# A two-block network on one core: products in passes, a new entrance, and reordered closing norms

## The reference, cut to what matters

```python
# first block
hn = rmsnorm(concat(meta, x), norm1_g)
u, q, k, v, g_ssm, g_att = split(hn @ w_in)            # 1024 -> 512 + 3*512 + 2*1024
y_ssm = s5_mixer(u, ...)                               # 32 groups, 64 complex states each
q, k = rmsnorm(q), rmsnorm(k)
y_att = rmsnorm(diff_attention(q, k, v, lam, slopes))
h = h + (sigmoid(g_ssm) * (y_ssm @ w_ssm_out) + sigmoid(g_att) * (y_att @ w_att_out)) @ w_o
up = rmsnorm(h, norm2_g) @ w_up                        # 1024 -> 2 * 2816
h = h + (gelu(causal_conv3(up_a)) * up_b) @ w_down
# second block, on the 256 tokens of x
z = rms_norm(h, norm_mix) @ w_in_2                     # nine parts
ya, yb, yc = rglru(...), hgrn2(...), moba(...)
y = concat(rms_norm(ya), yb, rms_norm(yc))
x = x + y @ w_out_2
x = x + relu(rms_norm(x, norm_mlp) @ w_ff1) ** 2 @ w_ff2
return rms_norm(x, norm_final)
```

## Time and profile before

| | |
|---|---|
| median of 3 runs | 732.13 us (732.03, 732.13, 1547.2) |
| profiled execution | 735.88 us, of which the span of the core 734.1 us |
| TensorE busy | 706.6 us (96%), 6152 products and as many weight loads |
| VectorE busy | 537.2 us (73%) |
| ScalarE busy | 386.8 us (53%) |
| weights and inputs read | 113.69 MB, 16 DMA engines 48% busy with SP's queue |

### The profile page before, as it was taken

How to read it: one execution, slowest core, us unless ns; L and a number is a source line. 1 busy time by engine, 2 the same in 40 slices (tenths; PEclk the granted TensorE clock), 3 DMA queues, 4 the chain that set the end, 5 groups by cost and what they waited for, 6 DMA issues and landing times.

```text
span 734.1 us, 14582 instructions
## 1 busy us (share of the span) xinstructions
PE 706.6 (96%) x6152; PEld 663.5 (90%) x6152; DVE 537.2 (73%) x954; ACT 386.8 (53%) x587; POOL 24.3 (3%) x50
## 2 busy tenths in 40 slices
PE   6999999999999999999999999999889999999996
PEld 4988998888999999999999889888779998998995
DVE  5899798556978877776777889965767665666653
ACT  6487368366365454444446664587654434434431
POOL 3010000000000000000000320000000000000000
PEclk9999999999999999999999999999999999999999
DMA  8751153133555555555655553333346565565541
GB/s 241 207 171 59 59 172 117 60 112 119 172 173 173 185 200 190 173 177 196 199 175 173 179 172 116 116 115 116 115 125 194 190 210 172 184 215 175 179 165 57
DMA packets 94700, 115.66 MB, mean 158 GB/s; under 512 B 7971, under 2 KB 83932, under 8 KB 94636
## 3 DMA queue, kind: packets, MB, share of 16 engines
q1 hardware_dynamic: 94244, 114.51, 48.2%
q0 software_dynamic: 128, 0.13, 0.1%
q10 hardware_dynamic: 264, 0.10, 0.1%
HBM read 113.69 MB, written 1.05 MB: 156 GB/s over the span
## 4 chain that ended last, share of the span: by engine, by line
PE 78%; DVE 10%; ACT 7%; issue 3%; DMA 1%; SPq 0%; DVEq 0%; ACTq 0%
PE psum L1805 17%; PE psum L1806 16%; PE psum L1807 16%; PE psum L2344 4%; PE psum L2342 4%; PE psum L2343 4%; DVE w_lo L1081 4%; ACT w_hi L500 3%; PE psum L2111 2%; PE psum L2113 2%; PE psum L2109 2%; PE psum L1917 1%; PE psum L1952 1%; DMA xtok<-in_x_dram 1%; PE psum L2167 1%
## 5 line engine op out<-in xcount | busy, mean ns | idle before, releaser
L1081 DVE TENSOR_TENSOR w_lo<-w_raw,w_hi 128x2048 fp32r<-128x2048 f32 x105 | 239.4, 2288 | 72.0 <-ACT w_hi L500 71.8
L500 ACT ACTIVATE w_hi<-w_raw 128x2048 fp32r<-128x2048 f32 x105 | 199.0, 1906 | 54.4 <-PE psum L2344 36.6
L1805 PE MATMUL psum<-x2n_hi,w_hi 128*128 128x256 f32 x400 | 114.5, 286 | 2.6 <-DVE x2n_lo L1532 1.3
L1806 PE MATMUL psum<-x2n_lo,w_hi 128*128 128x256 f32 x400 | 112.0, 280 | 0.0
L1807 PE MATMUL psum<-x2n_hi,w_lo 128*128 128x256 f32 x400 | 111.9, 280 | 0.0
L1805 PE MATMUL psum<-hs_hi,w_hi 128*128 128x256 f32 (+1 forms) x352 | 99.5, 283 | 0.0
L1806 PE MATMUL psum<-hs_lo,w_hi 128*128 128x256 f32 (+1 forms) x352 | 99.1, 281 | 0.0
L1807 PE MATMUL psum<-hs_hi,w_lo 128*128 128x256 f32 (+1 forms) x352 | 98.9, 281 | 0.0
L1805 PEld LDWEIGHTS psum<-x2n_hi,w_hi 128*128 128x128 f32 x400 | 75.3, 188 | 5.9 <-DVE x2n_lo L1532 2.3
L1807 PEld LDWEIGHTS psum<-x2n_hi,w_lo 128*128 128x128 f32 x400 | 76.1, 190 | 0.0
L1806 PEld LDWEIGHTS psum<-x2n_lo,w_hi 128*128 128x128 f32 x400 | 75.2, 188 | 0.6
(11 more groups left out here) (439 smaller groups left out, 1520.8 us busy)
## 6 DMA issues: line engine op xcount, KB each, us to landing
w_raw<-in_w_ff_dram SPq DMA_DIRECT2D x32, 1024.0 KB, 5.3
w_raw<-in_w_in_dram SPq DMA_DIRECT2D x27, 1024.0 KB, 5.3
w_raw<-in_w_up_dram SPq DMA_DIRECT2D x22, 1024.0 KB, 5.1
w_raw<-in_w_down_dram SPq DMA_DIRECT2D x11, 1024.0 KB, 4.9
w_raw<-in_w_o_dram SPq DMA_DIRECT2D x4, 1024.0 KB, 5.4
w_raw<-in_w_out_dram SPq DMA_DIRECT2D x4, 1024.0 KB, 5.2
w_raw<-in_w_ssm_out_dram SPq DMA_DIRECT2D x2, 1024.0 KB, 5.1
w_raw<-in_w_att_out_dram SPq DMA_DIRECT2D x2, 1024.0 KB, 5.0
```

What stands on the lines that cost most here:

```text
L500: A.activation(w_hi[:, u % NW, :], raw[:, u % NRAW, :], ACT.Copy).then_inc(sem("hi_ready"), 1)
L1081: V.tensor_tensor(w_lo[:, u % NRAW, :], raw[:, u % NRAW, :], w_hi[:, u % NW, :].bitcast(F32), ALU.subtract).then_inc(sem("lo_ready"), 1)
L1805: T.matmul(out_, lh, rh, start=start, stop=False)
L1806: T.matmul(out_, lh, rl, start=False, stop=False)
```

## The change

1. **Passes.** `unit()`, `down()` and `ff2()` run through all slices with high x high, then all with high weight x low activation, then all with low weight x high activation. The wait for `lo_ready` moves from the start of the unit to the third pass of its first group; at the start stands `hi_ready`. Where an activation is awaited, the first pass waits for its high half slice by slice, the second for its low half. `out_first` keeps the old order.
2. **Entrance.** SP loads both halves of x before those of unit 0. ScalarE makes the squares of the 256 tokens (`x_square`), VectorE the copies out of PSUM (`x_meta`, `x_pair`). Unit 0 is done in two halves of its contraction, each over both groups. TensorE gets products of the identity with itself that nobody reads, three before the meta tokens and eight before the first unit (`keep_warm`). The table of Sqrt is loaded first, the exponentials of `log_dt` follow the norm, and `s5_angles` follows the scaling of `u`.
3. **Closing norms.** VectorE scales the four `mo` slices first, starts the reciprocal of `rst2` behind two of the `ycat_lo` slices, and makes the `xc` slices of `ycat_lo` before it scales `hgo`; ScalarE takes the second Silu behind the `xc` slices; TensorE runs `ya_stat` ahead of `hg_bc`.

```diff
@@ sync
             for h in range(2):
                 c = slice(512 * h, 512 * h + 512)
                 for t in range(2):
                     sp.dma_start(xtok[:, 1 + t, c], x[0, P * t:P * t + P, c]).then_inc(sem(f"x_in{h}"), 16)
+            for h in range(2):
                 sp.dma_start(raw[:, 0, 1024 * h:1024 * h + 1024].rearrange("p (k n) -> p k n", k=4),
...
@@ scalar, entrance
-            x_pair(0)
+            act.wait_ge(sem("constants"), CONSTANTS["small"])
+            A.activation(small[:, 1, 8:9], eps_col, ACT.Sqrt)
+            x_square(1, 0)
+            x_square(2, 0)
...
+            for kt in range(4):
+                x_high(kt)
             first_half(0)
+            for kt in range(4, KD):
+                x_high(kt)
+            first_half(1)
+            done[0] = 1
+            x_square(1, 1)
+            x_square(2, 1)
+            split_to(2)
+            act.wait_ge(sem("x_sum"), 1)
+            A.activation(small[:, 1, 0:3], small[:, 0, 8:11], ACT.Sqrt, bias=eps_col,
...
@@ vector, entrance
+            x_meta()
+            for i in range(4):
+                x_pair(i)
+            for kt in range(4):
+                xn_low(kt)
             first_half(0)
...
+            split_to(2)
+            dve.wait_ge(sem("x_rms"), 6)
+            scaled("u", 0, uT, 0)
+            s5_angles()
             s5_denominator()
-            dve.wait_ge(sem("x_rms"), 2)
-            scaled("u", 0, uT, 0)
             s5_lambda()
...
@@ tensor, unit
-                if un:
-                    pe.wait_ge(sem("lo_ready"), un + 1)
-                else:
-                    pe.wait_ge(sem("first_lo"), 1)
+                pe.wait_ge(sem("hi_ready" if un else "first_hi"), un + 1)
...
+                    for kt in range(kk):
+                        if ready and fresh:
+                            pe.wait_ge(sem(ready + "_hi"), kt + 1)
...
+                        product(wh, ah, kt, first=kt == 0)
+                    for kt in range(kk):
+                        if ready and fresh:
+                            pe.wait_ge(sem(ready + "_lo"), kt + 1)
+                        product(wh, al, kt)
+                    if fresh:
+                        pe.wait_ge(sem("lo_ready" if un else "first_lo"), un + 1)
+                    for kt in range(kk):
...
+                        last = product(wl, ah, kt, final=kt == kk - 1)
                     last.then_inc(sem("group_done"), 1)
...
+            def keep_warm(n):
...
+                for _ in range(n):
+                    T.matmul(banks[0][:, 0:P], ident[:], ident[:], start=True, stop=True)
...
+            keep_warm(8)
+            first_unit()
...
@@ vector, closing norms
             for p_ in range(4):
                 STT(out=mo[:, p_, :], in0=mo[:, p_, :], scalar=col("att_norm", p_), in1=rst3[:, :],
                     op0=ALU.mult, op1=ALU.mult).then_inc(sem("yc"), 1)
-                if p_:
-                    y_low(p_ - 1, 3 + p_, mo[:, p_ - 1, :])
-            y_low(3, 7, mo[:, 3, :])
+            for p_ in range(2):
+                y_low(p_, 4 + p_, mo[:, p_, :])
             dve.wait_ge(sem("ya_rms"), 1)
-            seq(V.reciprocal(rst2[:, :], rst2[:, :]))
+            mark(V.reciprocal(rst2[:, :], rst2[:, :]))
+            for p_ in range(2, 4):
+                y_low(p_, 4 + p_, mo[:, p_, :])
...
```

More of the change, by code:

```diff
@@ L1741, in _ @@
             for m in range(2):
+                y_low(4 + m, m, xc[:, m, :])
+            for m in range(2):
                 dve.wait_ge(sem("hg_bc"), m + 1)
@@ L1866, in _ @@
                     pe.wait_ge(sem(f"x_in{kt // 4}"), 32)
-                need(pe, "hT_copy", kt // 2 - 1)
-                to_features(kt).then_inc(sem("xT"), 1)
+                for t in range(2):
+                    c = 256 * (kt % 2) + P * t
+                    last = T.transpose(banks[4 + kt // 2][:, c:c + P], xtok[:, 1 + t, P * kt:P * kt + P], ident[:])
+                if kt % 2:
+                    last.then_inc(sem("xT"), 1)
             param_cols(1, "ssm_in", 4)
@@ L1878, in token_rows, with first_unit @@
                 return last
[L1880 removed]
+            def first_unit():
+                wh, wl = (w[:, 0, :].rearrange("p (k n) -> p k n", k=KD) for w in (w_hi, w_lo))
+                for h in range(2):
+                    for m in range(2):
+                        for n_, (w, x) in enumerate(((wh, xn_hi), (wh, xn_lo), (wl, xn_hi))):
+                            if m == 0 and n_ != 1:
+                                pe.wait_ge(sem((("first_hi", "hi_ready")[h], "", ("first_lo", "lo_ready")[h])[n_]), 1)
+                            for kt in range(4 * h, 4 * h + 4):
+                                if m == 0 and n_ < 2:
+                                    pe.wait_ge(sem(("xn_hi", "xn_lo")[n_]), kt + 1)
+                                last = T.matmul(banks[m][:, 0:TOK], w[:, kt, P * m:P * m + P], x[:, kt, :],
+                                                start=(kt == 0 and n_ == 0), stop=(kt == KD - 1 and n_ == 2))
+                        if h == 1:
+                            last.then_inc(sem("group_done"), 1)
+            keep_warm(8)
+            first_unit()
             pe.wait_ge(sem("C_ready"), 2)
@@ L2088, in _ @@
             for i in range(2):
-                unit("att_out", i, (yatt_hi, yatt_lo, 0, NQ), 4, ready=None if i else "yatt_lo")
+                unit("att_out", i, (yatt_hi, yatt_lo, 0, NQ), 4, ready=None if i else "yatt")
             for i in range(4):
-                unit("w_o", i, (mix_hi, mix_lo, 0, NQ), 8, ready=None if i else "mix_lo")
+                unit("w_o", i, (mix_hi, mix_lo, 0, NQ), 8, ready=None if i else "mix")
             def h1_stat():
@@ L2252, in yc_stat @@
                              stop=(p_ == 3)).then_inc(sem("yc_stat"), 1)
-            unit("hg_f", 0, x2n, 8, ready="x2n_lo")
+            unit("hg_f", 0, x2n, 8, ready="x2n")
             x2_stat()
@@ L2348, in ff2, with product @@
-                if not final:
-                    last.then_inc(sem("acc_unit_done"), 1)
+                def product(u_, w, kt, t, h, z=False):
+                    return T.matmul(banks[4 + 2 * t + h][:, :], u_[:, i % 2, kt, P * t:P * t + P],
+                                    w[:, kt, 512 * h:512 * h + 512], start=False, stop=z, skip_group_check=True)
+                pe.wait_ge(sem("hi_ready"), un + 1)
+                pe.wait_ge(sem("u_hi"), 2 * i + 2)
+                if final:
+                    pe.wait_ge(sem("u_lo"), 2 * i + 2)
+                    pe.wait_ge(sem("lo_ready"), un + 1)
+                    for t in range(2):
+                        for n_, (u_, w) in enumerate(((u_hi, wh), (u_lo, wh), (u_hi, wl))):
+                            for kt in range(2):
+                                for h in range(2):
+                                    last = product(u_, w, kt, t, h, n_ == 2 and kt == 1)
+                        last.then_inc(sem("ff2_done"), 1)
+                    return
@@ new lines, in ff2 @@
+                for n_, (u_, w) in enumerate(((u_hi, wh), (u_lo, wh), (u_hi, wl))):
+                    if n_ == 1:
+                        pe.wait_ge(sem("u_lo"), 2 * i + 2)
+                    if n_ == 2:
+                        pe.wait_ge(sem("lo_ready"), un + 1)
+                    for kt in range(2):
+                        for t in range(2):
+                            for h in range(2):
+                                last = product(u_, w, kt, t, h)
+                last.then_inc(sem("acc_unit_done"), 1)
```

163 lines of the change are left out of this document (63 added, 100 removed).

## The result

The changed kernel takes 738.22 us (median of 7 runs, 737.28 to 740.39) against 735.36 us for the kernel before. The ratio is **1.0059, 95% interval 1.0033 to 1.0085**: slower by 0.6%, far inside the 2%. Two of the six runs of the kernel before in this ratio are the quick ones of the prediction's base (732.03 and 732.13); the other four have a mean of 735.5, and against these the changed kernel's mean of 738.68 is 0.44% slower. Its profiled execution takes 739.99 us with a span of 738.2, against 735.88 and 734.1 before: +4.1 us.

What follows compares the result with a forecast made beforehand. TensorE, busy for 96% of the span, was taken as the bound; entrance +2.7, handovers +2.1 and closing norms -1.45 gave +3.4 us, from a run median of 732.13 to 735.5 us, range 727.5 to 739.5.

Steps and rivals of the forecast that it cites:

- the base: Starting time of the forecast: the runs' median, 732.13 us, taken as 3.75 us below the profiled execution's 735.88.
- rival A: Pace of 256-column products: passes lead them into the faster spacing, up to -10 us, giving 725.5 to 730; chance 0.16.
- Pace and count: TensorE's products throughout: passes keep the number of products and weight loads, and the spacing stays; 0 us.
- Order behind the norm: Entrance: VectorE's list 2.8 us later from unit 2's low half, so TensorE reaches unit `q` 1 later by 2.7 us.
- rival B: Hidden entrance: unseen slack or an early clock rise makes the entrance cost 0 to 1 us, sum 732 to 733.5; chance 0.22.
- Identity products: Ahead of meta tokens and unit 0: unit 0 starts later but ends at 22.0, against 22.1 before; 0 us.
- Handovers: Between stages: 17 products left behind the last high half; `mix` +0.8, `x3` +0.9, `x2n` +0.3, others +0.1; sum +2.1 us.
- Closing norms: Output projection: the last `ycat_hi` and the chain behind it, to TensorE's restart, come earlier; -1.45 us, bounds -0.5 and -2.5.
- Rival C: Transposes between units `q` 0 and `q` 1: clock falls to 1.2 GHz, +1.8 us and slower transposes, 737.5 to 740; chance 0.13.
- signs of being wrong: Unit `q` 1 before 53 us, one spacing only of 256-column products, or groups behind `mix` and `x3` ending no later.

Runs made afterwards that it cites:

- combo: Changed kernel with the old product order in the first group of six slice-by-slice units, and angles before scaling `u`, `rbc` copy behind the sines; ratio 0.9939.
- passes: Kernel before with only the products in passes (`unit`, `down`, `ff2`), old entrance and old closing norms; ratio 1.0058.
- slices: Changed kernel with the first group of the six units whose activation comes slice by slice in the old order, three products per slice; ratio 0.9966.
- angles: Changed kernel with VectorE's angles ahead of the scaling of `u` and ScalarE's copy of `rbc` behind the two sines; ratio 1.0024.
- norms: Kernel before with only the reordered closing norms (`y_low`, `hg_g`, `ya_stat`); ratio 0.9976.
- after: The changed kernel itself, with all three parts of the change, against the kernel before; 738.22 us, ratio 1.0059.
- entr: Kernel before with only the new entrance, everything ahead of unit `u` 1; ratio 1.0005.
- warm: Changed kernel with two unread products ahead of each wait for a high half, from the third on, in the first group of `hg_f`; ratio 1.0033.
- fill3: Changed kernel with unread products ahead of waits in three sparse groups, in `hg_f`, `ff1` and `w_o` (30 products); ratio 1.0023.
- pair: Changed kernel with first and second product of a slice together in the six slice-by-slice first groups, third pass behind all slices; ratio 1.0009.
- both: The kernel `combo` with six products per slice, including the unit's second group, in the first unit of `hg_f` and `ff1`; ratio 0.9934 to the kernel before.

## Why the prediction came out as it did

**The direction and the size of the change were about right, the number was not.** I had +3.4 us on the profiled execution: 739.3. It took 739.99. In the ratio, +0.46% lies inside the interval of the measured +0.59%. But I put the forecast at 735.5 us, and that is 2.7 us under the median of 738.22.

**The step that failed is the base**: "The runs' median lies 3.75 us lower (732.13)". It came from three runs of which two happened to be among the quickest of this kernel. Of 85 later runs of the kernel before, 11 lie under 733.3 us, and the medians are 735.3 to 735.8, 0.1 to 0.6 us under the profiled execution and not 3.75. With the base at these medians the same +3.4 us gives about 739. As I wrote it, the forecast is the time that the kernel before really has (735.36), so it says "no change" where the runs show +0.6%. What makes a quick run is probably the pace of rival A, in another way than I had it. Low-half pass of a `down` unit in the changed kernel and in `combo` (TensorE):
```profile
356.37 2.05 PE L2148 MATMUL psum<-ff_lo,w_hi 128*128 128x256 f32 x16
358.25 0.99 PE L2148 MATMUL psum<-ff_hi,w_lo 128*128 128x256 f32 x7
```
```profile
366.45 1.98 PE L2161 MATMUL psum<-ff_lo,w_hi 128*128 128x256 f32 x16
368.27 0.96 PE L2161 MATMUL psum<-ff_hi,w_lo 128*128 128x256 f32 x7
```
16 products in 1.88 us and in 1.82, with the same code for this stage: 0.1175 and 0.1138 each, the two spacings of the earlier trace rows. (I misread the counts there: 48 and 46 products overlap the windows, 46 and 44 begin in them. The 4% between them is right.) In `passes` and `combo` the stage from the second `down` unit to the last goes at the quick one and takes 133.4 us instead of 136.5, so TensorE is 3.15 us ahead at its end; in the twelve other profiles it goes at the slow one nearly throughout. The runs of `slices` lie at 730.0 (four) and 733 to 735 (eight), those of `angles` at 734.4 to 734.8 (four) and about 737.7 (seven): the same step. That a quick run without profile is one with the quick pace is inferred; what sets the pace is open. So is why the share of quick runs differs so much: 11 of 85 for the kernel before, none of 12 for `norms`, 6 of 8 for `combo`.

**Term by term.**

- *Pace and count, 0:* right for the change. No order of products brings the quick spacing (`after` has it where the kernel before has it, and it comes and goes between executions). Rival A in its form, that passes lead the products into the quick spacing, is out: twelve of fourteen profiles have the slow one, with passes and without. That a kernel shifts the odds of the quick pace is not excluded.
- *Order behind the norm, +2.7:* the mechanism holds, the size was off; +1.36 was measured, the bound that I gave for unit 0 ending at 20.7. The clock rose by 14.8 and not behind the start of unit 0 (`rbc` at 21.87 and not 23.2, low half of unit 2 at 27.07 and not 28.5, `bb` at 45.00 and not 46.3: each 1.3 to 1.4 early, so the chain between them was sized right). In `entr`, with a still earlier rise, the whole part is -0.10, and in `slices`, `warm` and `fill3` -0.15 to -0.56: then rival B's outcome holds, and it is the more frequent one in the profiles. "Identity products: 0" was wrong by that 1.4 us.
- *Handovers, +2.1:* the mechanism holds and this is the term most under-sized. By the table, everything between unit `q` 1 and the end but the norms is +4.96. `w_o` (+0.75, forecast +0.8) and `ff1` (+1.07, +0.9) were right. `up_b` was taken as free, since "the high halves come before TensorE needs them": the last of them comes 0.25 us late and 17 products stand behind it, +0.54. `hg_f` with the last `down` unit had +0.3 and is +2.67. The last high half comes 0.6 us later against the start of that unit (15.4 us behind it, 14.8 before), since in passes all banks of `down` are finished in its last pass. From there to the statistics it is 4.25 us before, 4.9 in `passes`, `warm` and `fill3`, where the clock stayed up, and 6.35 in the changed kernel: 0.7 for the products left and 1.4 for the clock, for which the sum had nothing here.
- *Closing norms, -1.45:* -2.27. The chain was right (table load and restart move by the same amount), the shift of the last `ycat_hi` was worked out too small.
- *Rival C, the falling clock:* I looked for it at the transposes and gave it 0.13. In the changed kernel's profile it was not there, but in a place that the change itself had made sparse. `entr`, whose products behind unit 0 are all in the old order, has a fall too, at 520.8 to 524.2 us, right behind a wait of 2.04 us for `ycat_lo`. It cost nothing: the output projection takes 29.15 us and took 29.13 before, since TensorE would have waited later in it anyway. At the transposes it did fall in `slices`, `fill3`, `pair`, `combo` and `both` (0.50 from about 48 to 51 us). In `combo` that cost little (6.75 us from the first turning to unit `q` 1, 6.62 in `angles` without a fall), since TensorE waits there anyway; in `pair`, where it lasted to 56, 8.16. The Trainium skill ("TensorE: Matmul & The Clock Gate", Part 4) says that transposes do not count as activity; these five traces agree with it, the six other profiles with this entrance, which have the same transposes at full clock, show that it need not fall.

The two errors that hid each other in the sum are the handovers (2.9 too little) and entrance with norms (2.2 too much). That +3.4 came so close to the +4.1 of the two profiles was luck, the more so as 1.4 us of the 4.1 are a fall of the clock and 1.36 a late rise, both of which other executions don't have. None of the three signs of being wrong came: unit `q` 1 starts at 54.17, both spacings are there, and the groups behind `mix` and `x3` end later. Rival B's sum was slightly off: 3.4 less 2.7 plus 0 to 1 is 732.8 to 733.8, not 732 to 733.5.

## What to carry to other kernels

Where an operand arrives slice by slice, finish all that a slice allows before waiting for the next: what counts is the number of products left behind the last slice, and a list of single products between waits can also lose TensorE's clock, for microseconds after the wait is over. Look at the granted clock of each stretch that a change makes sparse, not only where TensorE rests already. And take the base of a forecast from the profiled execution if the runs shown are few: here 3 us, as much as the change itself, lay between two ways in which the same program runs. For the same reason compare kernels group by group before adding up their ratios.

## What the runs showed of the hardware

- A fall of the granted clock to 0.50 lasts 3.4 us in the profiles (421.0 to 424.4, 548.7 to 552.1, 48.0 to 51.4), in two cases twice that, and costs 1.4 to 1.5 us if TensorE is not held up later anyway, and nothing where it is (`entr`, 520.8 to 524.2). It is not in each execution of the same code.
- The clock's first rise comes at 18.0 to 19.4 us with the old entrance (three profiles) and at 9.4 to 15.0 with the new one (eleven), where TensorE is busy from 4.3 us on. At the entrance the granted clock reads 1.00 from the start; the rise is read from the spacing of the products.
- Products of 256 columns begin 0.1134 or 0.1177 us apart with the same code and the same granted clock; those of 258 columns show one spacing, about 0.120, in all fourteen profiles. Over the `down` stage that is 3.15 us.
